# A new order for the mixer of a two-layer hybrid block on one core: attention from the first token half on, all products on VectorE, last query tile inside the output projection

## What is computed

```python
for l in range(DEPTH):                                  # 2
    mod = (silu(c) @ ada_w[l] + ada_b[l])               # 6 x 1024 numbers
    h = rms_norm(x, mix_pre_g[l]) * (1.0 + scale_m) + shift_m
    q, k, v, x_lru, gate = split(h @ w_in[l])           # 512, 128, 128, 512, 512 columns
    q, k = apply_rope(q), apply_rope(k)
    # 8 query heads, 2 key heads, chunks of 64 tokens; each chunk sees itself and the one before;
    # softmax with one more logit per head (a sink)
    attn_out = sliding_window_attention(q, k, v, sinks)
    xc = causal_dwconv(x_lru, conv_w, conv_b)           # width 4
    r, i = sigmoid(xc @ w_a + b_a), sigmoid(xc @ w_x + b_x)   # block diagonal
    log_a = -8.0 * r * softplus(-lam)
    lru = scan(exp(log_a), sqrt(1 - exp(2 * log_a)) * (i * xc)) * gelu(gate)
    y = concat(rms_norm(attn_out, g_attn), rms_norm(lru, g_lru)) @ w_out
    x = x + gate_m * rms_norm(y, mix_post_g[l])
    ...                                                 # conv feed-forward, 1024 -> 6144 -> 1024
```

## Time and profile before

| | |
|---|---|
| median of 3 runs | 1294.04 us (1292.98 to 1294.46) |
| the profiled execution | 1294.48 us, span 1292.6 us |
| TensorE (PE) busy | 1177.5 us, 91% |
| VectorE (DVE) busy | 855.9 us, 66% |
| ScalarE (ACT) busy | 536.7 us, 42% |
| GpSimd (POOL) busy | 56.6 us, 4% |
| HBM | 152.64 MB read, 120 GB/s over the span |
| mean granted TensorE clock | 0.958 of full speed |

### The profile page before, as it was taken

One profiled execution on the slowest core, in us unless ns is written; L12 is line 12 of the kernel. 1 busy time (PEld: TensorE's weight loads), 2 busy tenths in 40 slices (PEclk: granted clock), 3 DMA queues, 4 the chain that ended last, 5 costly groups with the idle time before them and its releaser, 6 DMA issues.

```text
span 1292.6 us, 15931 instructions
## 1 busy us (share of the span) xinstructions
PE 1177.5 (91%) x6534; PEld 1012.4 (78%) x6534; DVE 855.9 (66%) x1293; ACT 536.7 (42%) x756; POOL 56.6 (4%) x66
## 2 busy tenths in 40 slices
PE   5988859889899999999988986899999999999996
PEld 5876549788778888888988764888888888888895
DVE  6786877878776777777566866457864466445545
ACT  4265553445322442344334566344542244234430
POOL 1011130000000000000000023000000000000000
PEclk7989879899999999999999979899999999999998
DMA  9513136323576447743221312020433333333211
GB/s 363 215 61 113 49 114 204 140 79 134 179 244 228 147 147 239 240 147 122 82 67 41 107 33 82 1 98 1 147 99 98 98 98 98 98 97 94 94 58 66
DMA packets 44936, 155.76 MB, mean 121 GB/s; under 512 B 5056, under 2 KB 7360, under 8 KB 44864
## 3 DMA queue, kind: packets, MB, share of 16 engines
q1 hardware_dynamic: 44720, 154.23, 35.5%
q10 hardware_dynamic: 144, 0.52, 0.1%
HBM read 152.64 MB, written 2.10 MB: 120 GB/s over the span
## 4 chain that ended last, share of the span: by engine, by line
PE 65%; DVE 22%; ACT 7%; DMA 3%; issue 3%; SPq 0%; DVEq 0%; ACTq 0%
PE ps L1626 65%; DVE sb_wL L1019 3%; DMA sb_raw<-in_w 3%; DVE sb_y L1078 2%; DVE sb_xc L1255 1%; DVE sb_R L1357 1%; ACT sb_wH L586 1%; DVE sb_y L1304 1%; DVE sb_x L1082 1%; ACT sb_R L757 1%; ACT sb_sq L683 1%; DVE sb_stage L1025 1%; DVE sb_y L1101 1%; DVE sb_tiny L1220 1%; DVE sb_adaw L1025 1%
## 5 line engine op out<-in xcount | busy, mean ns | idle before, releaser
L1626 PE MATMUL ps<-sb_hH,sb_wH 128*128 128x512 f32 (+1 forms) x1184 | 425.5, 365 | 19.9 <-DVE sb_wL L1019 8.8
L1626 PE MATMUL ps<-sb_hH,sb_wL 128*128 128x512 f32 (+1 forms) x1184 | 418.9, 360 | 0.0
L1626 PE MATMUL ps<-sb_hL,sb_wH 128*128 128x512 f32 (+1 forms) x1184 | 397.4, 360 | 3.9 <-DVE sb_hL L1108 3.9
L1626 PEld LDWEIGHTS ps<-sb_hH,sb_wH 128*128 128x128 f32 x1184 | 229.4, 194 | 60.6 <-DVE sb_wL L1019 10.3
L1626 PEld LDWEIGHTS ps<-sb_hH,sb_wL 128*128 128x128 f32 x1184 | 229.2, 194 | 32.3
L1019 DVE TENSOR_TENSOR sb_wL<-sb_raw,sb_wH 128x1024 fp32r<-128x1024 f32 x174 | 212.8, 1228 | 58.9 <-ACT sb_wH L586 58.5
L586 ACT ACTIVATE sb_wH<-sb_raw 128x1024 fp32r<-128x1024 f32 x174 | 181.9, 1051 | 154.8 <-DMA sb_raw<-in_w 154.8
L1626 PEld LDWEIGHTS ps<-sb_hL,sb_wH 128*128 128x128 f32 x1184 | 215.4, 193 | 37.0 <-DVE sb_hL L1108 4.7
L1626 PE MATMUL ps<-sb_mL,sb_wH 128*128 128x256 f32 (+1 forms) x608 | 206.6, 340 | 20.6 <-DVE sb_mL L1313 20.3
L1626 PE MATMUL ps<-sb_mH,sb_wH 128*128 128x256 f32 (+1 forms) x608 | 206.0, 339 | 5.9 <-ACT sb_mH L923 5.2
L1626 PE MATMUL ps<-sb_mH,sb_wL 128*128 128x256 f32 (+1 forms) x608 | 204.6, 337 | 0.0
(11 more groups left out here) (230 smaller groups left out, 1144.5 us busy)
## 6 DMA issues: line engine op xcount, KB each, us to landing
sb_raw<-in_w SPq DMA_DIRECT2D x174, 512.0 KB, 3.7
sb_adaw<-in_ada SPq DMA_DIRECT2D x48, 512.0 KB, 4.4
sb_stage<-in_ada SPq DMA_DIRECT2D x24, 512.0 KB, 11.2
sb_vw<-in_ada SPq DMA_DIRECT2D x24, 512.0 KB, 4.2
sb_side<-in_w SPq DMA_DIRECT2D x8, 512.0 KB, 4.9
sb_raw<-in_w SPq DMA_DIRECT2D x8, 384.0 KB, 14.2
sb_x<-in_x SPq DMA_DIRECT2D x4, 512.0 KB, 5.2
out<-sb_x SPq DMA_DIRECT2D x4, 512.0 KB, 2.9
```

Source lines behind the costliest of these rows:

```text
L1626: return nc.tensor.matmul(out, a, b, start=start, stop=stop, **kw)
```

## The change

The streams of the mixer are written out anew, operation by operation, with another order for each layer, and the pieces are moved as follows.

- Everything that GpSimd multiplied (`gated`, the probabilities, the products with the root, three products with the gelu) is on VectorE. GpSimd keeps only its constants and the softplus.
- Attention starts on the first half of the tokens: `scores_mm(0)` waits only for the ropes of half 0, and stands in the middle of the first x product in layer 0 and ahead of it in layer 1. `values` is in two halves. Most pieces of attention and gates stand in the middle of a product or just behind one.
- PSUM: gates always use banks 2 and 3, each tile waiting for the sigmoids of the one before; outputs use bank 4, which is also the first of the two banks of the transposes, so each `probs_transposed(t)` waits for `attn_low` of tile t - 1.
- `copy_out` is gone: `attn_high` and `attn_low` go by query tile and read the outputs from PSUM, in 128x128 pieces, four of each a tile.
- The transposes and outputs of the last query tile stand inside the output projection, behind its second and third chunk of the first half. Before its first half TensorE waits for tiles 0 and 1 only.
- The eight units have two buffers in place of four (in y), and are spread over the mixer; SyncE loads them in between the weight refills.
- Around the mixer: in three places low parts and splits move behind `x_update`, `x_squares` or `x_sums`; the splits and low parts of the second layer's chunks 6 and 7 move behind two more swaps and ropes. `lru_scaled` and `lru_low` alternate.

The diff, cut to its core:

```diff
-        ada_slots = [stage[:, 0, :], stage[:, 1, :], stage[:, 4, :], stage[:, 5, :],
-                     adaw[:, 0, :], adaw[:, 1, :], vwf]
+        ada_slots = [stage[:, 10, :], stage[:, 11, :], adaw[:, 0, :], adaw[:, 1, :], vwf]
...
+        GATE_BANKS = (2, 3)
+        O_BANK = 4
+        VALUE_BANK = [2, 3]
...
-            sp.wait_ge(ada_used, 4)
-            sp.wait_ge(shift_mm, 2)
-            for u in IN_UNITS[:4]:
-                ada_fill(u)
-            for n in range(GRP, 2 * GRP):
+            for n in range(GRP, GRP + 4):
+                refill(n)
+            sp.wait_ge(ada_used, 9)
+            ada_fill(IN_UNITS[0])
+            ada_fill(IN_UNITS[1])
+            for n in range(GRP + 4, 2 * GRP):
                 refill(n)
...
+                    if l == 0 and i == FIRST_G:
+                        unit_refill(IN_UNITS[2], IN_UNITS[0])
+                    if l == 0 and i == FIRST_G + 2:
+                        unit_refill(IN_UNITS[3], IN_UNITS[1])
+                        unit_refill(IN_UNITS[4], IN_UNITS[2])
                     if l == 0 and i == NPROJ - 1:
+                        for u in IN_UNITS[5:]:
+                            unit_refill(u, u - 2)
...
+                def attn_high(t):
+
+                    for j in range(AT):
+                        last = nc.scalar.activation(mH[:, j, t * P:(t + 1) * P], bank(O_BANK)[:, j * P:(j + 1) * P],
+                                                    ACT.Copy, scale=pcol(l, "g_attn", j))
+                    last.then_inc(attn_hi, 1)
...
+                def attn_low(t):
+
+                    dve.wait_ge(attn_hi, l * QT + t + 1)
...
+                    last.then_inc(attn_lo, 1)
```

More of the change, by code:

```diff
@@ L706, in decays, with root @@
                                          scale=spl[:, l, j:j + 1]).then_inc(aT_ready, 1)
+                def root():
+                    act.wait_ge(b2_ready, (l + 1) * LT)
+                    nc.scalar.activation(Rf, Rf, ACT.Sqrt).then_inc(root_ready, 1)
                 def exps(t):
@@ new lines, in _ @@
+                    copy_pt(2)
+                    decays(3)
+                    split_step(O0 + 3)
+                    gate_out(2)
+                    square_out(2)
+                    gelus()
+                    split_step(O0 + 4)
+                    attn_high(2)
+                    gate_out(3)
+                    root()
+                    split_step(O0 + 5)
+                    copy_pt(3)
+                    square_out(3)
+                    attn_high(3)
+                    lru_square(0)
@@ new lines, in _ @@
+                    rope(0, 0, 1)
+                    lo_chunk(B + 8)
+                    rope(0, 0, 2)
+                    lo_chunk(B + 9)
+                    rope(0, 1, 0)
+                    softmax(0)
+                    taps(0)
+                    lo_chunk(B + 10)
+                    rope(0, 1, 1)
+                    lo_chunk(B + 11)
+                    rope(0, 1, 2)
+                    lo_chunk(B + 12)
+                    taps(1)
+                    normalise(0)
+                    softmax(1)
@@ new lines, in _ @@
+                    gated(0)
+                    taps(2)
+                    lo_chunk(B + 13)
+                    taps(3)
+                    lo_chunk(O0)
+                    drives(0)
+                    normalise(1)
+                    softmax(2)
+                    lo_chunk(O0 + 1)
+                    attn_low(0)
+                    out_squares(0)
+                    gated(1)
+                    normalise(2)
+                    softmax(3)
+                    mod_unit(IN_UNITS[1])
@@ new lines, in _ @@
+                    gated(2)
+                    out_squares(1)
+                    mod_unit(IN_UNITS[2])
+                    attn_low(1)
+                    drives(1)
+                    gated(3)
+                    drives(2)
+                    mod_unit(IN_UNITS[3])
+                    lo_chunk(O0 + 2)
+                    drives(3)
+                    normalise(3)
+                    lo_chunk(O0 + 3)
+                    attn_low(2)
+                    out_squares(2)
+                    mod_unit(IN_UNITS[4])
@@ new lines, in _ @@
+                    lo_chunk(O0 + 4)
+                    drive(0)
+                    mod_unit(IN_UNITS[5])
+                    drive(1)
+                    lo_chunk(O0 + 5)
+                    mod_unit(IN_UNITS[6])
+                    drive(2)
+                    mod_unit(IN_UNITS[7])
+                    drive(3)
+                    scan(0)
+                    attn_low(3)
+                    scan(1)
+                    product(0)
+                    scan(2)
+                    product(1)
```

597 lines of the change are left out of this document (350 added, 247 removed).

## The result

The changed kernel takes 1246.67 us (median of 4 runs, 1244.63 to 1249.5) beside 1294.25 us: ratio 0.9633, 95% interval 0.9615 to 0.9651, or 47.6 us less. Five more runs of it gave 1246.38 us and 0.9635. The profiled execution took 1246.5 us. The forecast was 1248, range 1236 to 1270.

A forecast was written before the change was run, and what follows sets the result against it. No engine was full: a serial chain's latency bound the mixers, with VectorE the new bound after reordering. Gains 29.2 (layer 1) + 18.5 (layer 0) + 2.9 (joints) = 50.6; 1294.5 - 50.6 + 4 (half clock) = 1248 us, range 1236 to 1270.

The forecast's parts named there:

- Layer 1's mixer, 29.2 us: Layer 1, first x product to LRU half of the output projection: that half starts at 804.8 instead of 834.0.
- Its floor: Layer 1: if VectorE never idles, its 79.4 us of work end the LRU sums at 793.
- the signs: Expected in the new profile: VectorE 79 to 84 us from layer 1's first x product to LRU sums, gaps under 5.
- The prices on VectorE: Operation times assumed on VectorE: scans 1.2 us, tensor_scalar 0.43, probability products 1.2, other products 0.6, a 128-wide attn_low piece 0.27.
- the sum: VectorE's work in layer 1: 79.3 - 3 + 10.1 (products) + 1.2 (attn_low pieces) - 8.2 (waits beside GpSimd) = 79.4 us.
- Layer 0, 18.5 us: Layer 0's mixer: LRU half runs from about 187 instead of 205.8, despite VectorE waiting for the fourth unit's load.
- the walk: Operation-by-operation timing of both layers' mixers at full TensorE clock, each operation waiting for its last input; gains 29.2 and 18.5 us.
- The joints, 2.9 us: Low parts moved behind x_update and x_sums: 1.3 us gained in layer 0, 0.5 lost in layer 1, 2.1 gained between layers.
- Four us taken back for half clock: Both layers: one TensorE spell at the lower clock, 1.8 us a layer, 4 us subtracted from the gain.
- Latency: Rival, 0.25: in-order engines slip where they meet within 1 us, 12 us, plus four half-clock spells, 8 us: about 1268.
- The bank's turns: Rival "slower", 0.04: PSUM bank 4 makes each tile's transposes wait for attn_low, TensorE standing; at 8 us each about 1312.
- The better case (1238): Rival, 0.12: layer 0's unit loads come in time (4 to 6 us) and no half-clock spell stays (4 us).

## Why the prediction was right, point by point

- **Layer 1's mixer, 29.2 us: right.** The LRU half started 91.4 us after the first operation of the earlier trace rows's window, 29 us sooner than there; marks 2 to 3 give 30.0. The projection started 64.6 us after it (forecast 62.8), TensorE's wait before the transposes of tile 3 was 0.7 us (forecast 2.9), the LRU sums ended 80.4 us after it (forecast 81).
- **Its floor was the right number for half a reason.** I put VectorE's work at 79.4 us (79 to 84 among the signs) and called VectorE the new bound. It had 76.24 us of work, outside what I gave, and 4.2 of gaps, which meet the forecast's end. TensorE, with 78.97 us in the same 80.4, was as full, and the runs show that it is the one that counts in layer 1: less VectorE work gave nothing, 5 us of TensorE wait cost 5.2. In layer 0 the end hangs on VectorE's stream, and within it on the load of the fourth unit: 3.2 us more of TensorE wait cost nothing, 3.8 us less of VectorE's wait gave 3.8, and 4.9 us less of its work gave 1.5.
- **The prices on VectorE: right.** Scans 1.22 us (taken 1.2), tensor_scalars 0.43, attn_low in four pieces 1.0 to 1.1 us (taken 4 x 0.27). Over the whole run VectorE's busy time rose from 855.9 to 862.3 us, 3.2 a layer; the sum had 10.1 + 1.2 - 8.2 = 3.1.
- **Layer 0, 18.5 us: 2.6 too much at the end of it.** x and g products ended at 87.0, 93.0, 100.7, 108.7, 117.2, 128.7, 139.7 and 146.3, up to 1.7 us behind the walk; VectorE's wait for the fourth unit was 4.83 us (forecast 4.2), TensorE's for attn_low 2 4.5 us (4.4), but for attn_low 3 1.5 (5.3); 3.8 followed at the LRU sums. The LRU half began at about 187, as forecast. It then ran 12.2 us where it had run 9.7: 1.7 us are waits for low parts that VectorE makes one by one, and behind them a spell of the lower clock follows (at 191 us three matmuls of it take 0.64 us, at 195 us 0.36). 215.47 to 199.62 at its end is 15.9 us gained.
- **The joints, 2.9 us: about right or too little.** Removing them again cost 3.1 by the ratios and 4.4 by the medians. The wait of the earlier trace rows fell from 2.70 to 0.81, and the matmuls behind it no longer run a spell at half clock (24 of them in 2.95 us where it was 4.46), which I had not counted.
- **Four us taken back for half clock: one spell of the size taken, the count not shown.** Layer 1's mixer has one spell, behind the LRU sums, which costs 1.5 us in one profile of the changed kernel and is missing in the other. Layer 0's mixer, at a granted clock of 0.92, has the one named above. Both are already in the gains read at the ends of the mixers. A loss that I had not put down lies behind mark 3: 2.9 us, 1.8 of them in the window right behind it (24.67 us beside 22.85, granted clock 0.86 beside 0.93).
- **How the sum came out.** The mixers gave 15.9 + 29.0 = 44.9 us where the forecast had 18.5 + 29.2 - 4 = 43.7; the other places up to mark 3 gave 5.9 where it had 2.9 for the joints; behind mark 3 2.9 were lost where it had nothing. So 47.9 beside 46.6: the mechanism and the large terms are right, and that the total came within 1.3 us is in part luck.
- **The rivals.** Latency did not come back: no TensorE wait over 5 us in either mixer, and none over 1 us in layer 1's. The bank's turns stayed below products but for 1.4 and 4.5 us in layer 0 and 0.7 in layer 1. The better case (1238), with the loads in time, is the one that a load moved by one chunk comes near: 1241.5 us.
- **What the sum could not say.** It prices the move of the products as 10.1 us of VectorE work added and 8.2 saved. The runs agree that this is nearly even in the new order (VectorE is busy for 862.3 us with them and 857.9 without, 2.2 a layer), and add that in the old one it costs 0.4%: there TensorE waits longer for score tiles and probabilities.

## What to carry to other kernels

When no engine is full and all are waiting in turn, the order in which their work is issued can hold a large gain (47 us here); which engine does a product hardly mattered (nothing that can be told here, and a loss of 0.4% where the order was kept). Three pieces of the order were tested by themselves: a start of attention 5 us later (5 us lost), the last tile inside the projection (4) and the joints (3 to 4). What carries the other 35 us or so was not tested piece by piece. After such a change ask of each stage by itself which engine it runs to: take work from one and delay another, and read a mark at the end of the stage; here two layers of the same code had different answers. Count from the stage's own start, since what lies ahead of it moves the mark too. When buffers are cut from four to two, look at where each load can first be issued: one load moved up by a chunk was worth 4 to 5 us.

## What the runs showed of the hardware

Two things I had not expected. With equal waits, TensorE's clock can differ from one profile to another. Two profiles of the changed kernel, from the LRU sums of layer 1 to mark 3, each behind a wait of 0.75 us:

```profile
772.53:813.62 41.09, 41.09 (x331) 40.97 (x332) 18.01 (x32) 15.07 (x24) 0.00 (x0) 0.96 0.23 78
```
```profile
774.07:813.63 39.56, 39.56 (x331) 39.51 (x332) 18.01 (x31) 15.06 (x24) 0.00 (x0) 1.00 0.24 81
```

The same 331 matmuls take 41.09 us in one and 39.56 in the other: 1.5 us of a difference between two kernels can be nothing but the clock. The window behind mark 3, of the changed kernel and of the one without probability products, whose code is the same there:

```profile
813.62:838.29 24.67, 20.31 (x139) 18.96 (x139) 21.39 (x41) 12.06 (x21) 0.00 (x0) 0.86 0.00 1
```
```profile
812.13:835.19 23.06, 18.95 (x139) 17.59 (x139) 21.46 (x40) 12.06 (x21) 0.00 (x0) 0.93 0.00 1
```

The same 139 matmuls, with the same three longest waits (1.5, 1.4, 0.9 us), take 20.31 us in one and 18.95 in the other. And the 16 switches of table set that the sigmoids cause, 21.4 us of ScalarE's busy time over the run, moved the total by only about 1.3 us.
